# Block products for the outer merge gate: moving a projection out of the scan stage of a hybrid mLSTM and pooling layer

## The reference, cut to what matters

```python
parts_x = _split_proj((_rmsnorm(x, norm_w) * (1 + scale) + shift) @ in_w)   # q k v o z_m gates p z_p g_branch
h_x, _, _ = _bi_mlstm(qx, kx, vx, lix, lfx, st_f, st_b)      # chunks of 128 tokens, 4 heads, 2 directions
y_m = (norm(h) * head_norm_w * sigmoid(o) * silu(z_m)) @ branch_m_w
y_p = (((box_means(p) - p) @ pool_w) * pool_scale * silu(z_p)) @ branch_p_w
g_m, g_p = jnp.split(parts['g_branch'], 2, axis=-1)
merged = (sigmoid(g_m) * y_m + sigmoid(g_p) * y_p) @ out_w
out = _rmsnorm(x + gate * merged, final_norm_w)
```

## Time and profile before

| what | value |
|---|---|
| device time, three runs | 2357.16 us median (2351.56 to 2358.52) |
| profiled execution | 2348.31 us, its span 2346.5 us |
| TensorE busy in the span | 2238.0 us |
| VectorE, ScalarE, GpSimd busy | 1580.7, 972.2, 643.1 us |
| mean granted clock of TensorE | 0.981 |
| moved by DMA | 497.44 MB |

### The profile page before, as it was taken

How to read it: one execution, slowest core, us unless ns; L and a number is a source line. 1 busy time by engine, 2 the same in 40 slices (tenths; PEclk the granted TensorE clock), 3 DMA queues, 4 the chain that set the end, 5 groups by cost and what they waited for, 6 DMA issues and landing times. The chain is left out here.

```text
span 2346.5 us, 34856 instructions
## 1 busy us (share of the span) xinstructions
PE 2238.0 (95%) x11979; PEld 1894.1 (81%) x11979; DVE 1580.7 (67%) x2697; ACT 972.2 (41%) x1942; POOL 643.1 (27%) x557
## 2 busy tenths in 40 slices
PE   7799999998999999889999998999999899999998
PEld 5588888786788888778888887888888688887888
DVE  5554567857576675468878885888877655656564
ACT  6333345435333333334444444444444344352532
POOL 0233344542343443222322321232222102020200
PEclk9899999999999999999999999999999999999999
DMA  9466588768476754568777779777677664757562
GB/s 277 147 157 169 175 235 253 226 159 228 118 187 187 206 173 129 161 217 279 249 244 262 257 254 318 258 266 243 222 260 276 213 206 153 239 161 239 163 217 94
DMA packets 405441, 497.44 MB, mean 212 GB/s; under 512 B 25832, under 2 KB 291604, under 8 KB 400788
## 3 DMA queue, kind: packets, MB, share of 16 engines
q1 hardware_dynamic: 334740, 377.76, 48.7%
q10 hardware_dynamic: 62688, 83.90, 14.2%
q0 software_dynamic: 7840, 33.56, 5.0%
HBM read 348.63 MB, written 159.07 MB: 216 GB/s over the span
## 5 line engine op out<-in xcount | busy, mean ns | idle before, releaser
L1929 PE MATMUL bank<-xlate,wh 128*128 128x512 f32 x1536 | 503.5, 399 | 7.8 <-DVE v_t L2065 4.9
L1032 PE MATMUL bank<-xlate,wh 128*128 128x512 f32 x1280 | 409.1, 395 | 4.8 <-DVE wl L1309 4.0
L1929 PEld LDWEIGHTS bank<-xlate,wh 128*128 128x128 f32 x1536 | 281.3, 190 | 60.3 <-DVE v_t L2065 5.3
L1032 PE MATMUL bank<-xtop,wh 128*128 128x512 f32 x960 | 306.7, 397 | 5.9 <-ACT wh L1084 5.0
L1929 PE MATMUL bank<-xlate,wl 128*128 128x512 f32 x768 | 306.2, 399 | 0.0
L1032 PEld LDWEIGHTS bank<-xlate,wh 128*128 128x128 f32 x1280 | 238.9, 189 | 57.8 <-issue 6.3
L1032 PE MATMUL bank<-xlate,wl 128*128 128x512 f32 x640 | 251.7, 393 | 0.0
L1032 PEld LDWEIGHTS bank<-xtop,wh 128*128 128x128 f32 x960 | 178.6, 189 | 45.4 <-issue 7.9
L1337 DVE SCALAR_TENSOR_TENSOR tmp<-bank,psum 128x512 f32<-128x512 f32 x144 | 99.0, 688 | 144.6 <-PE bank L1032 103.9
L1032 PE MATMUL bank<-xtop,wl 128*128 128x512 f32 x480 | 189.2, 394 | 0.0
L1929 PEld LDWEIGHTS bank<-xlate,wl 128*128 128x128 f32 x768 | 145.6, 190 | 25.6
(11 more groups left out here) (334 smaller groups left out, 5332.6 us busy)
## 6 DMA issues: line engine op xcount, KB each, us to landing
v_t<-vk_d SPq DMA_DIRECT2D x144, 384.0 KB, 3.7
qk_d<-os SPq DMA_DIRECT2D x32, 1024.0 KB, 4.9
q_t<-qk_d SPq DMA_DIRECT2D x128, 256.0 KB, 4.1
wraw<-wpair_d ACTq DMA_DIRECT2D x23, 1024.0 KB, 7.0
rawb<-in_in_w_dram ACTq DMA_DIRECT2D x80, 256.0 KB, 5.4
wraw<-in_in_w_dram ACTq DMA_DIRECT2D x76, 256.0 KB, 4.0
vk_d<-os SPq DMA_DIRECT2D x16, 1024.0 KB, 4.4
k_t<-qk_d SPq DMA_DIRECT2D x64, 256.0 KB, 5.2
```

What stands on the lines that cost most here:

```text
L1032: mm = pe.matmul(dst[:, :], a[:, kd, :], x_block(part, XB[name])[:, kd], start=(kd == 0 and n == 0), stop=(kd == KH - 1 and n == 2))
L1929: mm = pe.matmul(bank[m % 2][:, :], a[:, u % 2, k, :], xlate[part][:, BLOCK_OF[k // KH, tq], k % KH], start=(k == 0 and n == 0), stop=(k = ...
```

## The change

The projection for g_m moves from the scan stage to the projection stage. UNITS gets four units of kind "m" for each half of the tokens, which go the way of the "p" units: seven block products each, tanh by ScalarE into a slot of os, a store by SP, here to gm_d. UA and what is planned from it move along. The scan stage keeps the kinds "o" and "z": 64 pieces, with shares of 10 for the slots up to step 62 and 12 after it. Its pair copies wpair_d go from 12 to 8. The scores of the next step follow each of four consecutive matmuls.

With it go these edits of the scan stage. num times 1/den of the first 64 steps is made by ScalarE (`normalise`) in the slot after. The output is stored from three slots (HS, the third in num_more). tanh_z has two buffers, and gstage is gone. GpSimd's turns after the eighth wait for p_lo, the count of low parts of the weights p, in place of step_done. The pooling gate zpq is loaded in four parts, each as soon as its z piece has been stored.

```diff
-SCAN_COLS = [off + 2 * P * n for off in (O0, Z0, GM0) for n in range(KT // 2)]
+SCAN_COLS = [off + 2 * P * n for off in (O0, Z0) for n in range(KT // 2)]
...
-UNITS = [(0, i, kind) for kinds in ("vk", "qs", "p") for i in range(HEADS) for kind in kinds]
+UNITS = [(0, i, kind) for kinds in ("vk", "qs", "p", "m") for i in range(HEADS) for kind in kinds]
 UNITS += [(1, 0, kind) for kind in "qs"] + [(1, i, kind) for i in range(HEADS) for kind in "vk"]
-UNITS += [(1, i, kind) for i in range(1, HEADS) for kind in "qs"] + [(1, i, "p") for i in range(HEADS)]
+UNITS += [(1, i, kind) for i in range(1, HEADS) for kind in "qs"] + [(1, i, kind) for kind in "pm" for i in range(HEADS)]
...
-return kind_of(a) == "p"
+return kind_of(a) in "pm"
...
-sp.dma_start(gp_d[2 * i + e, :, t0:t0 + TQ], s_slot(which)).then_inc(s_stored[which], 16)
+sp.dma_start((gm_d if kind == "m" else gp_d)[2 * i + e, :, t0:t0 + TQ], s_slot(which)).then_inc(s_stored[which], 16)
...
-c0 = {"q": Q0, "k": K0, "v": V0, "p": GP0}[kind] + i * HD
+c0 = {"q": Q0, "k": K0, "v": V0, "p": GP0, "m": GM0}[kind] + i * HD
...
-QS, KS, VS, SS = 4, 3, 4, 4
+QS, KS, VS, SS, HS = 4, 3, 4, 4, 3
...
-tanh_z = sb("tanh_z", [P, TQ])
+tanh_z = sb("tanh_z", [P, 2, TQ])
+num_more = sb("num_more", [P, TQ])
 ustage = sb("ustage", [P, 2, TQ])
-gstage = sb("gstage", [P, 2, TQ])
...
-pw_loaded = sem("pw_loaded"); zpq_loaded = sem("zpq_loaded"); mixq_loaded = sem("mixq_loaded")
+head_loaded = sem("head_loaded"); zpq_loaded = [sem(f"zpq_loaded{n}") for n in range(2)]; 
...
-g_stored = [sem(f"g4_stored{n}") for n in range(2)]
+h_made = sem("h_made")
...
-KINDS = "ozm"
+KINDS = "oz"
...
-ng = [sum(p[2] == "m" for p in PIECES[:m]) for m in range(NPI + 1)]
...
-cut = [t * NPI * NMM // NSLOT for t in range(NSLOT + 1)]
+SHARE = [10 if t < LEAD + NHALF - 1 else 12 for t in range(NSLOT)]
+cut = [sum(SHARE[:t]) * NPI * NMM // sum(SHARE) for t in range(NSLOT + 1)]
...
+def num_of(l):
+    return num[:, l % HS] if l % HS < 2 else num_more[:, 0:VW]
...
-    elif kind == "m":
-        sp.wait_ge(act_read, na[m] + 1)
-        sp.dma_start(gm_d[trip % (NTRIP // 2) * 2 + e, :, t0:t0 + TQ],
-                     gstage[:, ng[m] % 2, :]).then_inc(g_stored[ng[m] % 2], 16)
+def first_zp(m):
+    trip, u, kind, e, tq = PIECES[m]
+    if kind == "z" and trip == NTRIP - 1:
+        g = 2 * e + tq
+        sp.dma_start(zpq[:, g], zp_d[g, :, QUARTERS[0] * TQ:(QUARTERS[0] + 1) * TQ]).then_inc(zpq_loaded[tq], 16)
...
-    sp.wait_ge(fin, 4 * (l + 1))
+    sp.wait_ge(h_made, l + 1)
     dst = h_d if l < NHALF else hsum_d
-    sp.dma_start(dst[latent_chunk(l), :, h * HD:(h + 1) * HD], num[:, l % 2, 0:HD]).then_inc(h_stored[l % 2], 16)
+    sp.dma_start(dst[latent_chunk(l), :, h * HD:(h + 1) * HD], num_of(l)[:, 0:HD]).then_inc(h_stored[l % HS], 16)
...
-    sp.wait_ge(h_stored[f % 2], 16 * (f // 2 + 1))
+    sp.wait_ge(h_stored[f % HS], 16 * (f // HS + 1))
...
+first_zp(m)
...
-        sp.dma_start(pw[:, :, :], pool_w[0].rearrange("g c n -> c g n")).then_inc(pw_loaded, 16)
+        sp.dma_start(pw[:, :, :], pool_w[0].rearrange("g c n -> c g n")).then_inc(head_loaded, 16)
...
-        sp.dma_start(mixq[:, :, :], mix_d[:, :, QUARTERS[0] * TQ:(QUARTERS[0] + 1) * TQ].rearrange("g p t -> p g t")).then_inc(mixq_loaded, 16)
-    if t == HEAD_AT + 4:
-        sp.wait_ge(u_made, nz[-1])
-        sp.dma_start(zpq[:, :, :], zp_d[:, :, QUARTERS[0] * TQ:(QUARTERS[0] + 1) * TQ].rearrange("g p t -> p g t")).then_inc(zpq_loaded, 16)
+        sp.dma_start(mixq[:, :, :], mix_d[:, :, QUARTERS[0] * TQ:(QUARTERS[0] + 1) * TQ].rearrange("g p t -> p g t")).then_inc(head_loaded, 16)
 for m in ending(NSLOT - 1):
     store_piece(m)
+    first_zp(m)
...
-    sp.wait_ge(g_stored[n], 16 * ng[-1] // 2)
-sp.wait_ge(h_stored[NL % 2], 16 * NL // 2)
+for n in range(HS):
+    if n != (NL - 1) % HS:
+        sp.wait_ge(h_stored[n], 16 * len(range(n, NL, HS)))
...
-if 0 <= l + 1 < NHALF and i % 2 == 1 and 2 <= i // 2 < 2 + len(SCORES):
-    if i == 5:
+if 0 <= l + 1 < NHALF and i >= 3 and i - 3 < len(SCORES):
+    if i == 3:
         scores_ready(l + 1)
-    score(l + 1, i // 2 - 2)
-if t < LEAD and i % 8 == 7 and i // 8 < CPS - 1:
+    score(l + 1, i - 3)
+if t < LEAD and i % 5 == 4 and i // 5 < CPS - 1:
...
-        if nz[m] >= 1:
-            act.wait_ge(z_read, nz[m])
-        act.activation(tanh_z[:, :], bank[m % 2][:, :], ACT.Tanh, scale=0.5).then_inc(dz, 1)
-    else:
-        a = ng[m]
-        if a >= 2:
-            act.wait_ge(g_stored[a % 2], 16 * (a // 2))
-        act.activation(gstage[:, a % 2, :], bank[m % 2][:, :], ACT.Tanh, scale=0.5).then_inc(act_read, 1)
+        if nz[m] >= 2:
+            act.wait_ge(z_read, nz[m] - 1)
+        act.activation(tanh_z[:, nz[m] % 2, :], bank[m % 2][:, :], ACT.Tanh, scale=0.5).then_inc(dz, 1)
+def normalise(l):
+    act.wait_ge(fin, 3 * l + 3)
+    act.activation(num_of(l)[:, 0:HD], num_of(l)[:, 0:HD], ACT.Copy, scale=den[:, l % 2, 1:2]).then_inc(h_made, 1)
...
+if 0 <= l - 1 < NHALF:
+    normalise(l - 1)
...
-if t == HEAD_SPLIT - 1:
-    act.wait_ge(pw_loaded, 16)
+if t == HEAD_SPLIT:
+    act.wait_ge(head_loaded, 32)
...
-    act.wait_ge(mixq_loaded, 16)
...
-        act.wait_ge(fin, 4 * (l - 1) + 1)
+        act.wait_ge(fin, 3 * (l - 1) + 1)
...
-dve.scalar_tensor_tensor(out=ustage[:, a % 2, :], in0=tanh_z[:, :], scalar=1.0, in1=bank[m % 2][:, :],
+dve.scalar_tensor_tensor(out=ustage[:, a % 2, :], in0=tanh_z[:, a % 2, :], scalar=1.0, in1=bank[m % 2][:, :],
...
+if l >= HS:
+    dve.wait_ge(h_stored[l % HS], 16 * (l // HS))
 if l >= 2:
-    dve.wait_ge(h_stored[L], 16 * (l // 2))
-dve.scalar_tensor_tensor(out=num[:, L, :], in0=XBANK[:, 0:VW], scalar=col(d, c, 1, h),
+    dve.wait_ge(h_made, l - 1)
+to = num_of(l)
+dve.scalar_tensor_tensor(out=to, in0=XBANK[:, 0:VW], scalar=col(d, c, 1, h),
                          in1=ysb[:, :], op0=ALU.mult, op1=ALU.add).then_inc(fin, 1)
-dve.wait_ge(fin, l * 4 + 1)
-dve.scalar_tensor_tensor(out=den[:, L, 0:1], in0=num[:, L, HD:HD + 1], scalar=col(d, c, 2, h),
-                         in1=num[:, L, HD + 1:HD + 2], op0=ALU.max, op1=ALU.max).then_inc(fin, 1)
-dve.wait_ge(fin, l * 4 + 2)
+dve.wait_ge(fin, l * 3 + 1)
+dve.scalar_tensor_tensor(out=den[:, L, 0:1], in0=to[:, HD:HD + 1], scalar=col(d, c, 2, h),
+                         in1=to[:, HD + 1:HD + 2], op0=ALU.max, op1=ALU.max).then_inc(fin, 1)
+dve.wait_ge(fin, l * 3 + 2)
 dve.reciprocal(den[:, L, 1:2], den[:, L, 0:1]).then_inc(fin, 1)
-dve.wait_ge(fin, l * 4 + 3)
-if l < NHALF:
-    dve.tensor_scalar(num[:, L, 0:HD], num[:, L, 0:HD], den[:, L, 1:2], None, ALU.mult).then_inc(fin, 1)
-else:
+if l >= NHALF:
+    dve.wait_ge(fin, l * 3 + 3)
     dve.wait_ge(h_back[L], 16 * ((l - NHALF) // 2 + 1))
-    dve.scalar_tensor_tensor(out=num[:, L, 0:HD], in0=num[:, L, 0:HD], scalar=den[:, L, 1:2],
-                             in1=hother[:, L, :], op0=ALU.mult, op1=ALU.add).then_inc(fin, 1)
+    dve.scalar_tensor_tensor(out=to[:, 0:HD], in0=to[:, 0:HD], scalar=den[:, L, 1:2],
+                             in1=hother[:, L, :], op0=ALU.mult, op1=ALU.add).then_inc(h_made, 1)
...
-    pool.wait_ge(step_done, NCS - 8 + turns[0])
-pool.memset(state[:, :, :, :], 0.0).then_inc(state_zero, 1)
+    if turns[0] <= 8:
+        pool.wait_ge(step_done, NCS - 8 + turns[0])
+    else:
+        pool.wait_ge(p_lo, turns[0] - 8)
+pool.memset(state[:, :, :, :], 0.0).then_inc(mask_made, 1)
 pool.memset(cmask[:, :, :], 0.0).then_inc(mask_made, 1)
-pool.wait_ge(mask_made, 1)
+pool.wait_ge(mask_made, 2)
...
-if g == 0:
-    dve.wait_ge(zpq_loaded, 16)
+dve.wait_ge(zpq_loaded[g % 2], 32)
```

More of the change, by code:

```diff
@@ L667, in hybrid_block @@
             S_AT = {"C22": (0, 0), "C11": (0, 1), "C21": (1, 0), "C12": (1, 1)}
-            npool = [sum(UNITS[b][2] in "sp" for b in range(u)) for u in range(NU + 1)]
+            npool = [sum(UNITS[b][2] in "spm" for b in range(u)) for u in range(NU + 1)]
             def s_slot(which):
@@ L1127, in staged @@
                                 act.wait_ge(g_stored[g], 16)
-                        elif UNITS[u - 1][2] in "sp":
+                        elif UNITS[u - 1][2] in "spm":
                             for other in S_AT:
@@ L1638, in hybrid_block @@
             x_back = [[sem(f"x_back{n}_{j}") for j in range(KT // 2)] for n in range(2)]
-            setup = sem("setup"); state_zero = sem("state_zero"); mask_made = sem("mask_made")
+            setup = sem("setup"); mask_made = sem("mask_made")
             s_done = sem("s_done"); s_copied = sem("s_copied"); w_exp = sem("w_exp")
@@ L1643, in hybrid_block @@
             y_read = sem("y_read"); nm_masked = sem("nm_masked"); fin = sem("fin"); state_new = sem("state_new")
-            h_stored = [sem(f"h_stored{n}") for n in range(2)]
+            h_stored = [sem(f"h_stored{n}") for n in range(HS)]
             h_back = [sem(f"h_back{n}") for n in range(2)]
@@ L1895, in step @@
                     if l >= 1:
-                        pe.wait_ge(fin, 4 * (l - 1) + 1)
```

(7 more changed lines are left out.)

## The result

The changed kernel takes 2380.12 us (median of four, 2370.22 to 2384.91) where the kernel before took 2355.80 on the same chip: a ratio of 1.0106, 95% interval 1.0085 to 1.0127, slower by some 25 us. The forecast was 2349, a little faster. The profiled execution took 2378.40 us, against 2348.31 before: 30 us more, where the steps of the forecast gave 8 less. Some 6 of the 30 are the choice of executions, as the medians are 24 us apart, so single terms are good to a few us.

A forecast was written before the change was run, and what follows sets the result against it. TensorE was taken to set the pace, with VectorE nearly equal in the shorter scan slots. Added 152.8 us less 160.9 saved in the scan gave -8 from 2357.2: 2349 us, range 2328 to 2380.

The forecast's parts named there:

- units, rebuild (first scan matmul): Before the scan: eight added units of 19.23 us, 153.8, less 3 for fewer pair copies in the rebuild unit.
- steps 0 to 58: Scan slots fall from 6.27 to 4.83 us, saving 83.5 us over 58 slots.
- steps 58 to 120: Scan: 56 slots fall from 5.81 to 4.83 us, saving 54.9; six reload slots save 7.2.
- last seven steps: End of scan, without state update: slots fall from 5.00 to 3.95 us, saving 7.3 us.
- Rival (3): VectorE becomes the scan's clock, by the port or ScalarE's longer chain: slots of 5.04 us, 2373 us, slower; chance 0.22.
- The prediction's own sign: The prediction is wrong if the mean scan slot is outside 4.7 to 5.0 us.
- GpSimd's turn ... so a later turn costs nothing: Scan: GpSimd's turn waits for p_lo; only work awaited by the final stage stands behind it, cost 0 until the last slots.
- carried over this way: Scan: mean slots of before, small losses included, less removed matmuls at 0.229 us each, give 4.75 us by TensorE.
- The sentence on collisions that come back on den or ek_l: Scan: if collisions return on den, ek_l or state_l, VectorE needs 4.76 + 0.28 = 5.04 us a slot, the upper end.
- between 0 and 24 us, I take 12 again: Scan, where x blocks are reloaded: 12 us were lost before; the same loss was taken again, range 0 to 24.
- rival (4): Transfers: the losses in the scan's reload stretch double to 24 us, 2361 us; chance 0.15.
- needed a slot later ... covered by that distance: SP's queue in the scan: h store about 1 us later, other direction's load behind it needed a slot later; cost 0.

The follow-up runs named there:

- the run with the multiply: Changed kernel with the multiply by 1/den of the first 64 steps back on VectorE: 2390.22 us, ratio 1.0149 to the kernel before.
- half the bytes: Changed kernel with each of the 16 reload transfers of the x blocks cut to half its bytes, still eight in one slot: 2366.19 us, ratio 1.0061.
- spreading: Changed kernel with the x blocks' reload issued two transfers a slot over four slots for each half, same bytes: 2371.84 us, ratio 1.0086.
- equal shares: Changed kernel with SHARE 11 in every slot instead of 10 and 12, reload at steps 59 to 67 planned: 2368.65 us, ratio 1.0054.

## Why the prediction was wrong

In the profiled executions, term by term:

| step of the forecast | forecast | measured | miss |
|---|---|---|---|
| units, rebuild (first scan matmul) | +150.8 | +155.7 | 4.9 |
| lead | -8 | -6.6 | 1.4 |
| steps 0 to 58 | -83.5 | -72.8 | 10.7 |
| steps 58 to 120 | -62.1 | -49.3 | 12.8 |
| last seven steps | -7.3 | -2.1 | 5.2 |
| boundary and final stage | +2 | +5.2 | 3.2 |
| sum | -8.1 | +30.1 | 38.2 |

The first row is from these matmuls, of the kernel before and of the changed one:

```profile
985.29 0.79 PE L1929 MATMUL bank<-xlate,wh 128*128 128x512 f32 x1 [4.91 <-DVE v_t L2065]
```

```profile
1141.01 0.79 PE L1933 MATMUL bank<-xlate,wh 128*128 128x512 f32 x1 [5.04 <-DVE v_t L2069]
```

**What held.** The unit's 19.23 us, to the hundredth. TensorE's new pace: 4.75 forecast, 4.76 measured in steps 80 to 112. p_l near 0.3 us. Rival (3), VectorE as the steady clock at 5.04, did not occur in steady slots; its bound was right in kind, as the run with the multiply shows (half of 0.35 us a slot visible). The prediction's own sign was a mean slot outside 4.7 to 5.0: steps 0 to 58 took 5.01 in the mean, and 4.80 without the pooling arithmetic.

**The step that failed first: "GpSimd's turn ... so a later turn costs nothing".** I looked for who waits for GpSimd and not for what its overdue turns do to VectorE. Pooling costs the scan 20.6 us now and cost 9.1 before: 11.5 us of the miss, shown by the two runs without it. The means of before held the small loss; "carried over this way" assumed that it would stay small. It doubled, although the new pacing had all but removed it in the longer slots (1.2 us). What is left to explain the difference is the slot, shorter by 1.5 us: more turns are overdue after a change of group, and VectorE has less time in which to catch up. The other edits of the change were not varied one by one. The sentence on collisions that come back on den or ek_l spread that price evenly over the slots. It fell in three places.

**The step "between 0 and 24 us, I take 12 again".** The reload lost 23 us (60.9 less 8 x 4.76), which is the size of rival (4). A sum of bytes shows part of it. The stretch moved 18.0 MB (60.9 us at 295 GB/s); at the 382 to 392 GB/s that the kernel before reached in its reload, that takes 46 us, 8 more than eight slots of 4.76. The slots of before were each 1.0 to 1.5 us of gate matmuls longer, time in which transfers ran. But the stretch was not full throughout (share 0.84, the first eight transfers were partly over before it), and with half the bytes it still lost 11.7 us. The rest is the place in the queue: "needed a slot later ... covered by that distance" did not hold behind eight transfers (12.65 us of waiting for hother, 8.22 behind eight half ones); spreading gave 6 us back, equal shares 7 in the stretch. How the 23 us divide between bytes and place stays open.

**The last seven steps** saved 2.1 instead of 7.3 us, and step 122 alone took 6.8. There ScalarE waited for the load of mixq at the head of its queue, ysb stood behind it, and VectorE's num waited for ysb:

```profile
1825.06 0.63 ACT L2053 ACTIVATE pw_h<-pw 128x512 fp32r<-128x512 f32 x1 [1.42 <-DMA mixq<-mix_d]
```

```profile
1826.52 0.48 DVE L2155 SCALAR_TENSOR_TENSOR num<-bank,cols,ysb 128x258 f32<-128x258 f32 x1 [2.55 <-ACT ysb L2061]
```

This was read in the trace, not tested.

**The first row.** The rebuild unit stayed at 31.6 us by its M1 copies, so the 3 us for fewer pair copies did not come; 1.9 us more lie scattered over the other units. The 3.2 us of the boundary and the final stage were not traced to a cause and are within what executions differ by. Neither was tested.

**The new pacing was mis-sized, too low.** Valued at 0.28 us a slot, 32 us over the scan, it is worth 44 in the changed kernel and 10 by itself on the kernel before. So the change without it is worse than it looks: the move of the gate with its other edits costs some 25 + 10 = 35 us against the kernel before with the new pacing. What the move had to win, 22 us of fewer matmuls (96 x 0.229: 768 in the scan against 672 in the units), was lost to a scan whose slots are too short to hide the rest.

## What to carry to other kernels

When work leaves a stage that it bounded, price the losses that it hid. List each wait and each burst there, and ask what it costs with the shorter slot, instead of carrying the mean over. An engine whose results nobody waits for can still be the cause, if it works in arrears beside one that shares its memory port: start its pieces where the neighbour does not use the port, and let it never catch up. For a block of transfers, add up the bytes of the stretch and divide by the best rate that the trace shows: that is the least it takes. Then look at which small load with a near deadline stands behind the block.

## What was not expected of the hardware

In the kernel before, the multiply of num by a column, which has one wide SBUF input and needs 0.35 us alone, took 1.70 us beside GpSimd's pieces:

```profile
1315.09 1.70 DVE L2157 TENSOR_SCALAR num<-num,den 128x256 f32<-128x256 f32 x1
```

And den, whose tensor inputs are single columns, took 0.62 in place of 0.22 us. So the size and the number of the wide inputs do not tell which operations are held; of those seen here, the ones that read PSUM were spared. TensorE's granted clock was 0.50 (1.2 GHz, the lower level) from 1550 to 1560 us, in and behind the wait of 12.98 us, and 0.82 in the ten us after, so that a stall of VectorE costs TensorE more than its length:

```profile
1550.00:1560.00 10.00, 2.23 (x10) 2.26 (x11) 6.38 (x15) 3.29 (x8) 1.28 (x1) 0.50 0.90 314
1560.00:1570.00 10.00, 10.00 (x49) 8.63 (x48) 6.63 (x17) 4.21 (x12) 2.58 (x2) 0.82 0.49 154
```
